# A two-block fp32 network on one core: the feed-forward stages and the last projection are joined to their neighbours, two norms work by halves, and in the even layer taps and transposes change places

## The reference

```python
# feed-forward of the first block (2816 channels = 22 tiles of 128)
fn = rms_norm(h, norm_ffn)
g  = fn @ ffn_w_gate
g_conv = ffn_conv_b + sum(cw[i] * g_pad[:, i:i+s] for i in range(3))
h  = h + (silu(g_conv) * (fn @ ffn_w_up)) @ ffn_w_down

# even layer: state-space branch a, 31-tap convolution branch b
proj = rmsnorm(x) @ w_in
xbc  = silu(causal_dwconv(xbc, conv_w, conv_b))           # 4 taps
y    = ssd_chunked(xs, dt, a, bs, cs)                     # 4 groups, in chunks of 128 tokens here
u    = causal_dwconv(glu_v * sigmoid(glu_g), dw_w, dw_b)  # 31 taps
x    = x + concatenate([y_a, y_b]) @ w_out

# odd layer: 8 heads of differential attention
q, k, v, gate = split(rmsnorm(x) @ w_in, 4)
w = softmax(q1 k1) - lam * softmax(q2 k2)
o = rmsnorm(w @ v) * (1 - lam_init)
x = x + (o * silu(gate)) @ w_out
```

## Time and profile before

| | us |
|---|---|
| median of 3 runs | 3430.79 (3429.12 to 3433.35) |
| the profiled execution, its own time | 3430.47 |
| its span in the trace | 3428.7 |
| TensorE busy | 3122.5 (91%) |
| VectorE busy | 1774.7 (52%) |
| ScalarE busy | 992.6 (29%) |
| GpSimd busy | 806.5 (24%) |
| TensorE's mean granted clock | 0.957 of full speed |

### The profile page before, as it was taken

How to read it: one execution, slowest core, us unless ns; L and a number is a source line. 1 busy time by engine, 2 the same in 40 slices (tenths; PEclk the granted TensorE clock), 3 DMA queues, 4 the chain that set the end, 5 groups by cost and what they waited for, 6 DMA issues and landing times. The chain is left out here.

```text
span 3428.7 us, 38871 instructions
## 1 busy us (share of the span) xinstructions
PE 3122.5 (91%) x15406; PEld 2455.8 (72%) x15406; DVE 1774.7 (52%) x2683; ACT 992.6 (29%) x1866; POOL 806.5 (24%) x478
## 2 busy tenths in 40 slices
PE   5999898878899999999899999998998999999769
PEld 3777777666587787787677777776676777777657
DVE  4233566543632133133558887888443267777751
ACT  2332344314222011011223233424222244444430
POOL 1221000250322323323222232323132221111002
PEclk9998999999899999999899999999998999999879
DMA  2112000010111111111211111121331100000012
GB/s 105 38 35 92 13 1 13 25 62 18 51 49 43 48 44 43 49 49 50 85 50 43 68 44 68 44 74 53 141 101 62 43 31 26 32 26 26 7 62 74
DMA packets 46715, 170.28 MB, mean 50 GB/s; under 512 B 5200, under 2 KB 5472, under 8 KB 45664
## 3 DMA queue, kind: packets, MB, share of 16 engines
q1 hardware_dynamic: 44832, 161.85, 13.9%
q0 software_dynamic: 1728, 6.29, 0.5%
HBM read 145.06 MB, written 23.07 MB: 49 GB/s over the span
## 5 line engine op out<-in xcount | busy, mean ns | idle before, releaser
L176 PE MATMUL acc<-x_hi,w_hi 128*128 128x512 f32 x2064 | 855.5, 414 | 66.8 <-DVE x_lo L267 43.4
L169 POOL CAST w_hi<-w_raw 128x1024 fp32r<-128x1024 f32 x217 | 237.9, 1096 | 2555.9 <-PE acc L178 1512.8
L177 PE MATMUL acc<-x_lo,w_hi 128*128 128x512 f32 x2064 | 829.8, 402 | 0.0
L178 PE MATMUL acc<-x_hi,w_lo 128*128 128x512 f32 x2064 | 829.0, 402 | 0.0
L171 POOL TENSOR_TENSOR w_lo<-w_raw,w_hi 128x1024 fp32r<-128x1024 f32 x217 | 543.3, 2504 | 17.4
L176 PEld LDWEIGHTS acc<-x_hi,w_hi 128*128 128x128 f32 x2064 | 396.2, 192 | 191.2 <-issue 59.6
L178 PEld LDWEIGHTS acc<-x_hi,w_lo 128*128 128x128 f32 x2064 | 396.4, 192 | 97.5
L177 PEld LDWEIGHTS acc<-x_lo,w_hi 128*128 128x128 f32 x2064 | 397.8, 193 | 89.0 <-issue 1.4
L2241 DVE SCALAR_TENSOR_TENSOR acc<-ev_upad,cols,acc 128x1024 f32<-128x1024 f32 x232 | 298.2, 1285 | 4.2
L378 DVE TENSOR_TENSOR h<-h,acc 128x1024 f32 (+1 forms) x40 | 48.8, 1221 | 317.3 <-PE acc L178 317.3
L176 PE MATMUL aux<-x_hi,w_hi 128*128 128x512 f32 x448 | 193.1, 431 | 1.6 <-POOL w_lo L171 1.6
(11 more groups left out here) (495 smaller groups left out, 4974.8 us busy)
## 6 DMA issues: line engine op xcount, KB each, us to landing
w_raw<-in_stream SPq DMA_DIRECT2D x217, 512.0 KB, 3.5
h<-in_x SPq DMA_DIRECT2D x16, 512.0 KB, 9.1
spill_h<-h SPq DMA_DIRECT2D x8, 512.0 KB, 5.2
spill<-ev_zst SPq DMA_DIRECT2D x8, 512.0 KB, 3.1
h_even<-spill_h SPq DMA_DIRECT2D x8, 512.0 KB, 7.8
ev_zr<-spill SPq DMA_DIRECT2D x8, 512.0 KB, 3.5
spill_h<-h_even SPq DMA_DIRECT2D x8, 512.0 KB, 5.3
h<-spill_h SPq DMA_DIRECT2D x8, 512.0 KB, 6.4
```

Of the source, the lines that this page charges most:

```text
L169: pool.tensor_copy(k.w_hi[slot][:], k.w_raw[slot][:]).then_inc(k.w_split, 1)
L176: pe.matmul(out, w_hi, x_hi, start=start, stop=False)
L177: pe.matmul(out, w_hi, x_lo, start=False, stop=False)
L178: return pe.matmul(out, w_lo, x_hi, start=False, stop=stop)
```

## The change

1. **Feed-forward joined.** One `block_ffn` takes the place of `block_residual("xa_o")`, the three `block_ffn_in` and the three `block_residual("ffn_down")`, so that six barriers lie inside it no longer; a `k.release()` (one barrier) ends it. The norm becomes `LateNorm`: x_hi and x_lo are made of h times the gain as each h tile arrives, and 1/rms (`root`) is multiplied in after the matmul, by DVE. For that ACT's copy of gate becomes a DVE product (L1773 after), and one more DVE product with root follows the one with up (L1782 after). The first gate tile and the first down tile of each part take their last k-tile at the end (`late_tile`); the matmuls with ones stand behind the first gate tile.
2. **Norm by halves** (`HalfNorm`, `first_two`) in even and odd layer: the scaling works in 16 pieces of 128x512, 1/rms is made per half, and the first two weight tiles go together, six product matmuls for each piece.
3. **Even layer, chunk.** On DVE the chunk's `taps(1)`, `mix`, `taps(2)`, `combine` becomes `taps(3)`, `mix`, `combine`.
4. **Even layer, groups 1 to 3.** `feed(17)` ahead of `turn_x` becomes `feed(21)`, and `feed(4)` between `turn_x` and `turn_b` stays in group 0 only.
5. **Last projection inside `block_diff`.** The contraction over heads 0 to 3 is 16 pieces of 12 product matmuls into `aux`, issued in the periods 5 to 7 of head 6 (one each) and 0 to 7 of head 7 (two each in 0 to 4, then one), each added to h by a DVE operation of 128x512. After the loop TensorE has 36 product matmuls of the upper contraction (heads 4 to 6), the last head's transposes, then 156 more. The h tiles are read back in three groups, and out is stored tile by tile as before.

```diff
@@ LateNorm, block_ffn (in place of block_ffn_in and four block_residual)
+    def high(self, act, j):
+        act.activation(self.x_hi[:, j, :], self.k.h[:, j, :], ACT.Copy, scale=self.gain_of(j)).then_inc(self.hi, 1)
+    def low(self, dve, j):
+        dve.wait_ge(self.hi, j + 1)
+        dve.scalar_tensor_tensor(self.x_lo[:, j, :], self.k.h[:, j, :], self.gain_of(j), self.x_hi[:, j, :].bitcast(F32),
+                                 ALU.mult, ALU.subtract).then_inc(self.lo, 1)
...
+                for qs in (range(kt - 1), range(kt - 1, kt)):
+                    for c in (0, HALF):
+                        for q in qs:
+                            if c == 0:
+                                pe.wait_ge(lo, count + q + 1)
+                            mm = product3(...)
...
-                act.activation(gate[:, 2:SEQ + 2], k.acc[:, a % 2, :], ACT.Copy).then_inc(k.acc_free[a % 2], 1)
+                    dve.tensor_tensor(gate[:, 2:SEQ + 2], acc[:, slot, :], root[:], ALU.mult).then_inc(k.acc_free[slot], 1)
...
-                dve.tensor_tensor(prod[:], conv[:], k.acc[:, (a + 1) % 2, :], ALU.mult).then_inc(s["producted"], 1)
+                    dve.tensor_tensor(conv[:], conv[:], acc[:, other, :], ALU.mult).then_inc(k.acc_free[other], 1)
+                    dve.tensor_tensor(conv[:], conv[:], root[:], ALU.mult).then_inc(s["producted"], 1)
@@ HalfNorm
+    def place(self, m):
+        return m % KD, slice(m // KD * HALF, (m // KD + 1) * HALF)
+    def on_tensor(self, pe):
+        for c in (0, HALF):
+            pe.matmul(self.k.aux[:, c:c + HALF], self.k.ones, self.early.acc[:, c:c + HALF], start=True, stop=True).then_inc(self.total, 1)
@@ first_two
+    for c in range(2):
+        for q in range(KD):
+            norm.wait_ready(pe, c, q)
+            for i in range(2):
+                mm = product3(pe, outs[i][c], ...)
@@ even layer, TensorE and DVE
-                    feed(17)
+                    feed(21)
...
-                feed(4)
+                if g == 0:
+                    feed(4)
...
-                    taps(1)
+                    taps(3)
                     if c + 1 < TT:
                         mix(g, c + 1)
                     arrive(n // 3)
-                    taps(2)
                     combine(g, c)
@@ block_diff
+        if h == H - 2:
+            return (t - 5, t - 4) if t >= 5 else (0, 0)
+        if h == H - 1:
+            first = 3 + 2 * min(t, 5) + max(t - 5, 0)
+            return first, first + (2 if t < 5 else 1)
...
+            def piece(m):
+                if m:
+                    pe.wait_ge(s["added"], m)
+                output(aux[:, 0:HALF], m // 4, m % 4 // 2, m % 2, range(4)).then_inc(...)
...
+            for r in range(2):
+                for c in range(2):
+                    output(rows[r][c], 4, r, c, range(3))
             turn_o(H - 1, 0)
             turn_o(H - 1, 1)
+            pe.wait_ge(s["od_lo"], 8)
...
+            def add_piece(m):
+                dve.tensor_tensor(k.h[:, j, cols], k.h[:, j, cols], aux[:, 0:HALF], ALU.add).then_inc(s["added"], 1)
@@ the program
-        block_residual(k, "odd_out", k.od_hi, k.od_lo, KD, store=out)
```

More of the change, by code:

```diff
@@ new lines, in block_ffn @@
+def block_ffn(k):
+    wa, wb = STREAM["xa_o"]
+    ga = [STREAM[f"ffn_gu{p}"][0] for p in range(len(FFN_PARTS))]
+    da = [STREAM[f"ffn_down{p}"][0] for p in range(len(FFN_PARTS))]
+    end = STREAM[f"ffn_down{len(FFN_PARTS) - 1}"][1]
+    first = [sum(FFN_PARTS[:p]) for p in range(len(FFN_PARTS))]
+    LAST = len(FFN_PARTS) - 1
+    o_hi, o_lo = k.x_hi, k.x_lo
+    x_hi, x_lo = k.at("x3_hi", 64, [P, KD, SEQ], F32R), k.at("x3_lo", 96, [P, KD, SEQ], F32R)
+    g_hi, g_lo = k.at("g_hi", 0, [P, FFN_PARTS[0], SEQ], F32R), k.at("g_lo", 32, [P, FFN_PARTS[0], SEQ], F32R)
+    squares = EarlySquares(k, "ffn")
+    gate = k.at("ffn_gate", 128, [P, SEQ + 2])
+    conv = k.at("ffn_conv", 132.25, [P, SEQ])
+    root = k.at("ffn_root", 136.25, [P, SEQ])
+    late = LateNorm(k, "fn", COLS["norm_ffn"], x_hi, x_lo, squares, root[:], k.aux)
+    k.squares = EarlySquares(k, "even")
+    reloaded, stored, summed = k.residual_sems
+    base, k.residuals = k.residuals * KD, k.residuals + 1 + len(FFN_PARTS)
+    names = "padded conved chain silued producted hi lo".split()
+    s = {n: k.own(f"ffn_{n}") for n in names}
+    acc = k.acc
@@ L1568, in _, with tile @@
         @block.tensor
         def _(pe):
[L1570 to L1576, removed]
+            def tile(x_hi, x_lo, kt):
+                return lambda n, slot, turn: linear_tile(k, pe, n, slot, turn, x_hi, x_lo, kt)
@@ new lines, in _ @@
+            over_tiles(pe, wa, wb, tile(o_hi, o_lo, XA_HEADS))
+            for p, tiles in enumerate(FFN_PARTS):
+                if p == 0:
+                    late_tile(ga[p], x_hi, x_lo, KD, late.lo, 0)
+                    late.on_tensor(pe)
+                    over_tiles(pe, ga[p] + 1, da[p], tile(x_hi, x_lo, KD))
+                else:
+                    over_tiles(pe, ga[p], da[p], tile(x_hi, x_lo, KD))
+                late_tile(da[p], g_hi, g_lo, tiles, s["lo"], first[p])
+                over_tiles(pe, da[p] + 1, da[p] + KD, tile(g_hi, g_lo, tiles))
@@ L1578, in _ @@
         @block.scalar
         def _(act):
[L1580 to L1585, removed]
-                act.activation(gate[:, 2:SEQ + 2], k.acc[:, a % 2, :], ACT.Copy).then_inc(k.acc_free[a % 2], 1)
[L1587 to L1591, removed]
+            load_log_exp(act)
@@ L1593, in _ @@
+            for j in range(KD):
+                act.wait_ge(summed, base + (1 + LAST) * KD + j + 1)
+                k.squares.square(act, j, k.h[:, j, :])
         @block.vector
         def _(dve):
-            if norm is not None:
-                norm.on_vector(dve)
-            step = Steps(dve, s["chain"], 2 * first_tile)
-            dve.memset(gate[:, 0:2], 0.0).then_inc(s["padded"], 1)
[L1599 to L1610, removed]
-                dve.tensor_tensor(prod[:], conv[:], k.acc[:, (a + 1) % 2, :], ALU.mult).then_inc(s["producted"], 1)
[L1612 to L1615, removed]
@@ L1616 @@
+            k.squares.add(dve, KD - 1)
+    k.release()
 G_, V_, Z_ = "g", "v", "z"
@@ L2919, in _ @@
             lower_output(H - 1)
-            dve.wait_ge(s["od_lo"], H)
+            for r in range(KD):
+                add_row(r)
     k.release()
```

299 lines of the change are left out of this document (243 added, 56 removed).

## The result

The changed kernel took 3327.49 us, median of 4 runs (3321.68 to 3332.32), against 3430.44 before: ratio 0.9698, 95% interval 0.968 to 0.9716. The forecast was 3309, range 3292 to 3330; so it was faster, as forecast, by 103 us where 121.7 were summed; the median lies inside the stated range, near its upper bound, and outside the forecast's own 3299 to 3319. A second series of the same kernel gave 3332.76 (5 runs, ratio 0.971, 0.9697 to 0.9723), which is above the range.

The account below looks back on a forecast made before the run. TensorE, busy 91% of the span, was taken as the bound, so only its idle or half-clock time could go. Gains 52.5 + 12.9 + 14.4 + 8 + 34.4 - 0.5 = 121.7 from 3430.5 gave 3309 us, range 3292 to 3330.

Parts of the forecast that it names:

- part 2: Even norm by halves: first product matmul about 10.1 us after the last one before; gain 12.9 us, bounds 9 to 15.
- part 1: Feed-forward joined: norm 26.7, barriers 18.1 and half clock some 8 us go; gain 52.5 us, bounds 48 to 54.
- the release: One more release with its barrier, booked in the sum as a cost of 0.5 us.
- its twin: Odd norm by halves, with no wait behind it on an evacuation: gain 14.4 us, bounds 10 to 16.
- Part 3: Even layer's chunk: moved taps shorten TensorE's wait for the combined state only in group 3, by 0.7 us.
- Part 4: Even layer's value transposes later: about half of 5.6 us per group returns at decays; 8 us with taps, bounds 0 to 13.
- Part 5: Last projection in heads 6 and 7: end gains 51.4, heads cost 3 and 14.0; net 34.4 us, bounds 25 to 42.
- Two of the signs: Signs in the profile after: head 7 takes 66 to 70 us, and 54 us from its end to the span's.
- that rival's: Heads 6 and 7: pieces wait for adds, head 7 is 12 us longer, gain 22, time 3321; chance 0.15.
- The transposes' gain: Even layer: what TensorE no longer waits before turn_x it waits at decays; gain 0, time 3317; chance 0.17.
- DVE did not bound: Joined feed-forward: DVE's seven operations per hidden tile bound it; at 30 us per tile, time 3476; chance 0.03.
- The clock did not fall: Long dense feed-forward, some 790 us: clock at 0.95 of full costs 40 us, time 3349; chance 0.04.

Follow-up runs that it names:

- pair_tail: Changed kernel with the last five k-tiles of the paired tiles' second half done for tile one, then tile two, in both norms; 3320.31 us (0.9678).
- taps_back: Changed kernel with the even layer's chunk as before: one tap, mix, two taps, combine; transposes stay late; 3325.57 us (0.9701).
- piece_split: Changed kernel with the last 3 of 12 product matmuls of each period's first piece, heads 6 and 7, between the weights' turning and use; 3320.12 us (0.9675).
- ffn_dve_12: Changed kernel with twelve more DVE products of gate with root per hidden tile, same result; one run, 3498.38 us.
- late_plain: Changed kernel with no k-tile kept for last in each part's first gate and first down tile; one run, 3337.89 us.

## Why the prediction was right, and where its sum was off

All five parts gained by the mechanisms told, but part 2 had a wait that was not foreseen, and the sum was 13 us too high (121.7 against 108.8 in the traces), and it was that close partly by luck. Parts 2 and 5 gave 10.1 and 6.6 us less than forecast and part 1 gave 2.4 less, while the even layer's groups and last chunks gave 6.4 more (12.5 + 1.9 for 8); the release (0.5) and the stretches left out (0.8) nearly cancel. The range held the median because it was drawn out to the rivals.

**Part 1** forecast 52.5, measured 50.1, of which 50 are shown by taking it back. The steps are as told: the barriers and the norm left no gap, x_lo at the first gate tile was 0.66 us late (0.6 forecast), the last g_lo came 7.5 us after its down tile's start (7.3 forecast), 0.9 us before it was wanted in the two shorter parts and 2.3 in the first. What is missing from 52.5 stands in the window after: 0.7 us idle, nearly all of it the wait for x_lo, and 1.7 us lost in a spell of half clock of 3.4 us at 845.5, right behind the barrier wait of 2.6 that lies before the window. The kernel before has that spell too (at 844.9), and the change does not touch it; the sum took all of the half clock as gone. At full clock the window's matmuls are 786.1 us, as summed.

**Parts 2 and its twin** forecast 12.9 and 14.4; with the stretches behind 8.0 and 9.2 were measured, both below their bounds of 9 and 10. The step that failed is the pricing of the pair as if it ended when its matmuls end. Two tiles taken together free both weight buffers only at the end, so POOL's split of the third, 3.5 us, began 0.5 us before the pair's last matmul ended and stood uncovered:

```profile
1666.90 1.04 POOL L178 CAST w_hi<-w_raw 128x1024 fp32r<-128x1024 f32 x1 [25.87 <-PE acc L187]
...
1668.02 2.34 POOL L180 TENSOR_TENSOR w_lo<-w_raw,w_hi 128x1024 fp32r<-128x1024 f32 x1
...
1670.41 0.50 PE L185 MATMUL acc<-x_hi,w_hi 128*128 128x512 f32 x1 [2.95 <-POOL w_lo L180]
```

2.95 us in each norm and the half clock behind: 7.3 us in all, given back by pair_tail. The prediction counted what the new order needs to begin and not what it holds until its end. With pair_tail the two norms themselves gained 13.4 and 14.0, as forecast (of the odd one's 14.4 the prediction shows no sum); what is left are 1.7 and 1.2 us in the stretches behind them, where the changed kernel has spells of half clock (at 1732.9, and 6.83 us long at 2610.2) that the kernel before has not, or has shorter. The release was counted twice, in part 2's 10.1 us and as 0.5 in the sum; the barrier wait ahead of the even norm went from 4.36 to 4.98.

**Part 3** was right: nothing in groups 0 to 2, 1.0 us in the last chunks by taps_back (0.7 forecast).

**Part 4** forecast 7.3 without the taps, measured 12.5 and 12.7. Mechanism as told, the size of what comes back too large: 1.8 us of the 5.6 per group, where "about half" and a spell of half clock were booked.

**Part 5** forecast 34.4, measured 27.8 (29.0 less the 1.2 at the span's end). Two of the signs that the prediction named were missed: head 7 within 66 to 70 us, and 54 us from its end to the span's. Head 6 took 0.7 us more, where 3 were booked. Head 7 took 73.9, +20.1 in place of +14.0. The waits left were booked at 1.0 and were 5.0, all but 0.5 for the copy of the turned weights, as piece_split shows by removing them. The other 2.1 is TensorE's work. Thirteen pieces were booked, and the window holds 14, 2.8 us more, which are missing in head 6's; the 14 took 40.7 us, 1.5 over full pace; and the other matmuls took 28 us where 30.4 were booked. The end took 56.6 in place of 53.9: its steps up to the last head's output were as told, each beside the earlier trace rows; behind the wait of 3.54 came a spell of half clock (at 3275.8, 1.7 us lost) that the sum did not have, and from the last matmul to the span's end it took 5.6 where 4.4 were booked. Why these 1.2 were added is not shown.

```profile
3271.55 1.03 PE L2850 MATMUL aux<-mats,diff_osb 128*128 128x128 f32 x8
3272.26 1.41 DVE L3144 SCALAR_TENSOR_TENSOR o_diff<-aux,cols,o_diff 128x512 f32<-128x512 f32 x2 [6.23 <-PE aux L2850]
3273.76 1.06 ACT L3009 ACTIVATE od_hi<-o_diff 128x1024 fp32r<-128x1024 f32 x1 [8.98 <-DVE o_diff L3144]
3274.85 1.22 DVE L3149 TENSOR_TENSOR od_lo<-o_diff,od_hi 128x1024 fp32r<-128x1024 f32 x1 [1.18 <-ACT od_hi L3009]
3276.13 0.79 PE L185 MATMUL acc<-od_hi,w_hi 128*128 128x512 f32 x1 [3.54 <-DVE od_lo L3149]
```

The turning now starts 8.25 us after head 7's last matmul, since the 36 product matmuls stand ahead (DVE is idle for 6.23 before the gate); that was meant and is full work. The wait was 3.54 for 3.7 forecast.

**The rivals.** Head 7 did pay more than forecast, 6.1 of that rival's 12 us, but by waits for a copy, not for the adds: no wait for an add is in its list. The transposes' gain was not given back. DVE did not bound: in the loop it was at its slowest in most rounds and TensorE waited for nothing.

```profile
L1782 DVE TENSOR_TENSOR ffn_conv<-ffn_conv,ffn_root x22: 1225/3365/3365, 917.1 to 1555.5; 128x1024 f32<-128x1024 f32 x22
...
L1773 DVE TENSOR_TENSOR ffn_gate<-acc,ffn_root x22: 1225/1225/1227, 907.2 to 1543.0; 128x1024 f32<-128x1024 f32 x22
```

The product with two SBUF inputs takes 3.37 us at the median: 21 of the 22 began 0.12 us behind a POOL subtraction (L180) and ran beside it. The one with a PSUM input took 1.23 every time, beside POOL's cast in 21 rounds. In ffn_dve_12, where no POOL instruction runs beside the first of them, it took 1.22 or 1.23 all 22 times. That is what the rule of the Trainium skill ("GPSIMD Engine Reference", "1. Specifications") says; the trace agrees. The clock did not fall from 849 us to the feed-forward's last matmul.

**The last 6 us**, from the profiled execution's 3321.7 to the median, are in no term. The executions at the median were not traced; in the traces such differences lie mostly in the attention before the feed-forward.

## What to carry to other kernels

When two tiles are taken together so that a slow producer keeps up, ask what both hold until the end, and let one finish early. A wait of half a microsecond for a copy is filled by cutting the nearest independent product in two. An engine that waits anyway can take much more work, as long as it does not keep an accumulator longer than the other one takes to fill (16.3 us against 11.2 cost 5.2 each time, five products in place of one nothing). When pieces are counted into a window, cut the window where the pieces stand: here one piece, 2.8 us, fell into the next head's.

## What the runs showed of the hardware

With the order fixed, a stretch repeats to 0.2 us between executions, except for steps of about 1.6 us where one spell of half clock, 3.4 us in the records, falls in or not. Of four waits of 1.4 to 3.2 us in late_plain only one was followed by half clock. Of the 18 waits of 2.95 us for w_lo in the nine traces that have them, 17 were followed by one. In the unchanged attention, from 585 to 590 us on, some executions show no spell, some one of 3.4 us and others one of 17.1, with the same instructions; the stretch of some 80 us around it took 78.4, 80.1 and 86.1 us. Together with a second such place at 427 us (59.9 to 66.4) that is most of the spread between the traces of the changed kernel and its variants.

A DVE operation on one column can take as long as a whole one of POOL:

```profile
3200.72 2.40 POOL L180 TENSOR_TENSOR w_lo<-w_raw,w_hi 128x1024 fp32r<-128x1024 f32 x1
3200.76 2.38 DVE L3117 TENSOR_TENSOR diff_st<-diff_st,diff_lam 128x1 f32<-128x1 f32 x1
```

L3117 takes 0.16 us at the median; this one began just after POOL's and ended with it.
